# A two-block, four-layer forward pass: the join of the even and the odd layer in token halves, and three pieces of work moved off GpSimd

## What is computed

```python
for l in range(2):                       # first block
    hn = rms_norm(h, attn_norm[l])
    proj = hn @ w_in[l]
    mix = concat(rwkv7_mixer(...), retention_mixer(...), mla_mixer(...))
    h = h + mix @ w_out[l]
    h = h + ffn(rms_norm(h, ffn_norm[l]))
h = rms_norm(h, final_norm)
# second block
h = h + rms_norm(even_mixer(rms_norm(h, even_pre)) @ even_w_out, even_post)
h = h + rms_norm(odd_mixer(rms_norm(h, odd_pre)) @ odd_w_out, odd_post)
# odd_mixer begins with  rms_norm(h, odd_pre) @ odd_w_in   (q, k, v, gates)
```

## Time and profile before

| what | value |
|---|---|
| median of 3 runs | 2005.17 us (2004.16 to 2005.29) |
| profiled execution, its own time | 2005.63 us |
| its span, first to last instruction | 2003.8 us |
| PE busy | 1939.0 us, 97% |
| DVE / ACT / POOL busy | 1112.7 / 825.2 / 72.3 us |
| chain that ended last | PE 87%, DVE 9%, ACT 2%, issue 1%, DMA 1% |
| mean granted TensorE clock | 0.993 |

### The profile page before, as it was taken

How to read it: one execution, slowest core, us unless ns; L and a number is a source line. 1 busy time by engine, 2 the same in 40 slices (tenths; PEclk the granted TensorE clock), 3 DMA queues, 4 the chain that set the end, 5 groups by cost and what they waited for, 6 DMA issues and landing times.

```text
span 2003.8 us, 28013 instructions
## 1 busy us (share of the span) xinstructions
PE 1939.0 (97%) x11924; PEld 1558.9 (78%) x11924; DVE 1112.7 (56%) x1551; ACT 825.2 (41%) x1178; POOL 72.3 (4%) x47
## 2 busy tenths in 40 slices
PE   7998889999999999988999999999999999899998
PEld 6875678888888888647788888887788777689887
DVE  7568745543444544876544334447766674342474
ACT  4247524321222313774432222236554654335273
POOL 4010100000000000110000000000000000020000
PEclk9999999999999999999999999999999999999999
DMA  5340013223322323101122232233222222213102
GB/s 214 106 121 1 4 43 105 87 83 114 105 85 82 118 86 109 55 1 46 64 98 86 87 120 90 80 96 144 86 83 104 86 68 101 105 46 106 63 12 84
DMA packets 27500, 168.95 MB, mean 84 GB/s; under 512 B 3376, under 2 KB 3632, under 8 KB 12144
## 3 DMA queue, kind: packets, MB, share of 16 engines
q1 hardware_dynamic: 27376, 167.16, 24.2%
HBM read 161.77 MB, written 2.10 MB: 82 GB/s over the span
## 4 chain that ended last, share of the span: by engine, by line
PE 87%; DVE 9%; ACT 2%; issue 1%; DMA 1%; SPq 0%; POOL 0%; DVEq 0%; ACTq 0%; POOLq 0%
PE accumulators L698 25%; PE accumulators L700 25%; PE accumulators L699 25%; PE accumulators L724 4%; DVE ring_low L2072 1%; PE accumulators L838 1%; ACT ring_high L1514 1%; PE accumulators L980 1%; DVE accumulators L2318 1%; DVE arena L2331 1%; PE accumulators L946 1%; PE accumulators L929 1%; DVE arena L2382 1%; PE accumulators L1379 1%; DMA ring<-slabs_in 1%
## 5 line engine op out<-in xcount | busy, mean ns | idle before, releaser
L698 PE MATMUL accumulators<-arena_split,ring_high 128*128 128x512 f32 x2164 | 856.4, 396 | 22.1 <-DVE ring_low L2174 10.4
L699 PE MATMUL accumulators<-arena_split,ring_high 128*128 128x512 f32 x2164 | 845.0, 390 | 0.0
L700 PE MATMUL accumulators<-arena_split,ring_low 128*128 128x512 f32 x2164 | 844.9, 390 | 0.0
L698 PEld LDWEIGHTS accumulators<-arena_split,ring_high 128*128 128x128 f32 x2164 | 408.1, 189 | 117.4 <-issue 13.9
L699 PEld LDWEIGHTS accumulators<-arena_split,ring_high 128*128 128x128 f32 x2164 | 408.2, 189 | 87.8 <-issue 4.8
L700 PEld LDWEIGHTS accumulators<-arena_split,ring_low 128*128 128x128 f32 x2164 | 408.0, 189 | 85.5
L1514 ACT ACTIVATE ring_high<-ring 128x2048 fp32r<-128x2048 f32 (+3 forms) x161 | 281.3, 1748 | 414.1 <-PE accumulators L700 412.2
L2072 DVE TENSOR_TENSOR ring_low<-ring,ring_high 128x2048 fp32r<-128x2048 f32 (+3 forms) x161 | 338.5, 2103 | 186.0 <-ACT ring_high L1514 185.2
L1532 ACT ACTIVATE arena<-accumulators 128x512 f32<-128x512 f32 x72 | 43.1, 598 | 277.2 <-DVE accumulators L2053 277.2
L2053 DVE TENSOR_TENSOR accumulators<-accumulators,rstd 128x512 f32<-128x512 f32 x72 | 50.3, 698 | 119.2 <-PE accumulators L700 119.2
L2536 DVE TENSOR_TENSOR arena<-arena,accumulators 128x512 f32<-128x512 f32 x44 | 30.2, 687 | 119.7 <-PE accumulators L700 118.1
(11 more groups left out here) (357 smaller groups left out, 1764.7 us busy)
## 6 DMA issues: line engine op xcount, KB each, us to landing
ring<-slabs_in SPq DMA_DIRECT2D x115, 1024.0 KB, 4.8
ring<-slabs_in SPq DMA_DIRECT2D x38, 704.0 KB, 4.0
ring<-slabs_in SPq DMA_DIRECT2D x4, 576.0 KB, 3.7
h<-x_in SPq DMA_DIRECT2D x4, 512.0 KB, 7.5
con<-con_in SPq DMA_DIRECT2D x1, 2048.0 KB, 9.2
arena<-arena SPq DMA_DIRECT2D x8, 256.0 KB, 4.1
out<-arena SPq DMA_DIRECT2D x8, 256.0 KB, 2.0
ring<-slabs_in SPq DMA_DIRECT2D x2, 768.0 KB, 4.3
```

The costliest lines, as they stand in the source:

```text
L698: pe.matmul(out, weight[0], right[0], start=start, stop=False)
L699: pe.matmul(out, weight[0], right[1], start=False, stop=False)
L700: return pe.matmul(out, weight[1], right[0], start=False, stop=stop)
```

## The change

Four edits. At the start, ACT squares the eight input tiles and DVE adds them; POOL has no part in it, and ACT's copy of `in0_lo_mq0` stands before the second sine. The rotary key is spread to the heads by eight DMAs of SP, before the slab `out{l}_0`. In the decays, DVE makes the decayed keys in place of POOL, and the decayed queries move behind the first level's masked copies. At the joint, the last output tile and the first four odd groups are multiplied in halves of 256 tokens, and the squares, the norm's sum, root, parts and products go by halves; DVE and ACT prepare `odd_qk1` within the first half's tiles.

```diff
+        TOKENS = (slice(0, T // 2), slice(T // 2, T))
@@ PE, joint
-            for m in range(DT):
+            for m in range(DT - 1):
...
-            norm_sum("even_post")
+            def half_norm_sum(half):
+                ts = TOKENS[half]
+                pe.wait_ge(squares_summed, cnt.next(squares_summed))
+                b = group(("ss", "even_post", half), "act")
+                pe.matmul(b[:, ts], cst("ones"), A(51)[:, 0, ts], start=True, stop=True).then_inc(psum_ready, 1)
+            w = split_tiles(split_slab(f"even_out{DT - 1}"), 0, 2 * DT)
+            for half, ts in enumerate(TOKENS):
+                b = open_bank(("eo", DT - 1, half))
+                for n, k in enumerate(EVEN_ORDER):
+                    mm = product(b[:, ts], w[k], tuple(x[:, ts] for x in mix[k]), n == 0, n == 2 * DT - 1)
+                    if half and n == SUM_AFTER:
+                        half_norm_sum(0)
+                enter(("eo", DT - 1, half), "act")
+                mm.then_inc(psum_ready, 1)
...
             for k in range(DT):
                 parts_step(k)
                 for n in range(2):
-                    odd_product(n, k)
-                odd_product(*later.pop(0))
-            for n, k in later:
-                odd_product(n, k)
+                    odd_product(n, 0, k)
+                if k == 2:
+                    half_norm_sum(1)
+            later = [(n, half, k) for half in range(2) for k in range(DT) for n in (2, 3)]
+            for n, half, k in later[:2 * DT]:
+                odd_product(n, half, k)
+            del later[:2 * DT]
+            for k in range(DT):
+                parts_step(k)
+                for n in range(2):
+                    odd_product(n, 1, k)
+                if k < 4:
+                    odd_product(*later.pop(0))
+            for n, half, k in later:
+                odd_product(n, half, k)
-            pair("odd_qk2", [("qk", 4), ("qk", 5)], ["dve"] * 2, None, odd_norm_sum)
+            pair("odd_qk2", [("qk", 4), ("qk", 5)], ["dve"] * 2)
+            odd_norm_sum()
@@ ACT, start
+                    for m in range(DT):
+                        f(A(INPUT_SQUARES + m)[:, 0, :], h[:, m, :], ACT.Square).then_inc(cnt.up(input_square_ready), 1)
                     prepare(f"in{l}_k")
                     for n in range(2):
+                        if n:
+                            prepare(f"in{l}_v")
                         act.wait_ge(angle_ready, cnt.next(angle_ready))
...
-                    prepare(f"in{l}_v")
@@ ACT, joint
+            last_output(0)                                  # square and copy of one half
+            half_root(0)
             for m in range(DT):
+                odd_high(m, 0)                              # high part and square of one half tile
+                if m == 1:
+                    last_output(1)
+                if m == 2:
                     prepare("odd_qk0")
+                if m == 4:
+                    half_root(1)
             for m in range(DT):
+                odd_high(m, 1)
@@ DVE, start: after the first angle
+                        if n == 0:
+                            sum_input_squares()             # seven additions of 512 columns
@@ DVE, decays
                     tt(A(29, 2), A(29, 2), A(35, 2), MUL).then_inc(cnt.up(gram_inputs_ready), 1)
-                    tt(A(10, 2), A(10, 2), A(27, 2), MUL).then_inc(cnt.up(r_decayed), 1)
-                    dve.wait_ge(k_decayed, cnt.next(k_decayed))
+                    tt(A(12, 2), A(12, 2), A(35, 2), MUL).then_inc(cnt.up(k_decayed), 1)
...
+                def queries_decayed():
+                    tt(A(10, 2), A(10, 2), A(27, 2), MUL).then_inc(cnt.up(r_decayed), 1)
+                    retention_output(0)
-                spread_beside = {0: lambda: retention_output(0), 1: lambda: retention_output(1), 3: mixed_lows}
+                spread_beside = {0: queries_decayed, 1: lambda: retention_output(1), 3: mixed_lows}
@@ DVE, joint
+            last_square(0)
+            odd_input(0, {3: lambda: last_square(1), 4: lambda: prepare("odd_qk0")})
+            odd_input(1, {})
@@ POOL
-            for m in range(DT):
...
-                    pool.tensor_tensor(sq, h[:, m, :], h[:, m, :], ALU.mult).then_inc(cnt.up(pool_done), 1)
...
-                pool.tensor_copy(A(31, 8)[64:96], src.broadcast_to((32, 8, T))).then_inc(cnt.up(krope_spread), 1)
-                pool.tensor_tensor(A(12, 2), A(12, 2), A(35, 2), ALU.mult).then_inc(cnt.up(k_decayed), 1)
+            for half, ts in enumerate(TOKENS):
+                for m in range(1, DT):
...
@@ SP, before slab out{l}_0
+                if where is spread_slot:
+                    sp.wait_ge(psum_ready, finished(("rg", l, 1)))
+                    sp.wait_ge(krope_ready, l + 1)
+                    for hd in range(MLA_H):
+                        sp.dma_start(A(31 + hd)[64:96], A(30)[64:96]).then_inc(krope_spread, 16)
```

162 lines of the change are left out of this document (98 added, 64 removed).

## The result

| | before | after |
|---|---|---|
| median of 4 executions each, same chip | 2004.66 us (2003.70 to 2005.29) | 1994.02 us (1991.63 to 1996.54) |
| ratio | | 0.994, 95% interval 0.9923 to 0.9957 |
| profiled execution, its span | 2005.63, 2003.8 us | 1991.63, 1989.8 us |
| mean granted clock of the profiled one | 0.993 | 0.998 |

The change makes the kernel 10.6 us faster by the medians; the forecast was 7.3 us. The median lies in the recorded range (1992.5 to 2001.8) but under the forecast's own bracket of 1996 to 1999.6. The two profiled executions are 14.0 us apart, since the time of one and the same kernel moves by several microseconds with the mean granted clock of the execution, as the four times of after show. The experiments measure this.

What follows compares the result with a forecast made beforehand. TensorE, with work in flight for 97% of the span, was taken to bound the kernel. Terms -3.8-1.6-0.7-1.2 = -7.3 us, from 2005.63 less a further 0.46, gave 1997.8 us; forecast 1996 to 1999.6, range 1992.5 to 2001.8.

Steps and rivals of the forecast that it cites:

- rival 1: Decays: GpSimd's carried-key product doesn't collide with VectorE's L2399 and L2402; that part gives -4.1 us, total 1994.4 us; chance 0.20.
- B: Rotary keys at the beginning of attention: waits of 0.4 and 1.2 us go, -1.6 us (bounds 0 and -3).
- C: Decays, both layers: 2.05 us gained at the gram wait, 1.7 lost again per layer, -0.7 us (bounds -4.1 and 0).
- A: Start: the 2.06 us wait for in0_lo's split and 1.7 us of low-clock loss go, -3.8 us (bounds 0 and -4).
- D: Joint between even and odd layer: 10.7 us of idling and low clock becomes 9.5, -1.2 us (bounds -4 and +3).
- the cover of 4 us: Start: VectorE's split of in0_lo ends at 42.6 us, while PE wants it at 46.7 us.
- Rival 3: Start: VectorE, with seven more sums, still reaches in0_lo's split after 46.7 us; no gain there, 2001.6 us; chance 0.10.
- I take no more than the gaps: Attention: the keys' gain counted only as PE's first waits, 0.38 us in layer 0 and 1.21 in layer 1.
- the collision: Decays: GpSimd's 1.91 us carried-key product is released as L2399 starts and holds up L2402, costing 1.7 us per layer.
- The half matmuls: Joint: 256-column matmuls spaced 0.120 us, 0.0134 us of it fixed; 144 more of them cost +1.9 us.
- rival 4: Joint: slower, low clock until the four groups are done, a half matmul taking 0.213 us; up to 2012.9 us; chance 0.04.
- rival 2: Joint: another wait, longer low clock or weight loads replace the old wait; 0 to +3 us, 1999 to 2002 us; chance 0.16.

Runs made afterwards that it cites:

- the second comparison: The changed kernel itself measured again, nothing altered: median 1995.25 us, 11.5 us under the kernel before on the same chip.
- queries_last: The changed kernel with retention_output(0) ahead of the decayed queries: median 1991.39 us, 0.9919 of the kernel before.
- joint_only: The kernel before with only the token halves at the joint: median 2005.15 us, 0.9991 of the kernel before.
- no_joint: The changed kernel with the joint as before (whole tiles, one norm): median 1994.66 us, 0.9932 of the kernel before.
- sum_earlier: The changed kernel with the matmul of the first half's squares after the fourth instead of the eighth tile (SUM_AFTER 3 for 7): median 1993.88 us, 0.9929 of before.
- start_only: The kernel before with only the start's edit: median 2005.12 us, 0.9983 of the kernel before.
- no_keys: The changed kernel with the rotary keys spread by GpSimd's copy as before: median 1996.12 us, 0.9938 of the kernel before.

## Why the prediction was right, and where not

Sum of the edits by the stages: 4.0 + 3.7 + 1.8 + 1.1 = 10.6 us; the forecast had 3.8 + 1.6 + 0.7 + 1.2 = 7.3. That the medians of the first comparison differ by 10.6 too is luck to the tenth: the second comparison gave 11.5, and at equal clock it is 8.0. The time of 1994.0 lies within the range, not in the forecast's bracket, and near rival 1's 1994.4; rival 1 is not what happened. The 3.3 us between 7.3 and 10.6 are B's 2.1, C's 1.1 and A's 0.2, less 0.1 of D, and that their sum comes near rival 1 is luck.

- **A, the start: right.** 4.0 for 3.8. The two terms (the wait of 2.06 us and the low clock behind it) are both gone, and the cover of 4 us was there: VectorE's split was 0.25 us earlier than worked out. Rival 3 fell.
- **B, the keys: the largest miss, 2.1 us.** The step that failed is "I take no more than the gaps". PE's first waits in layer 0 were 0.38, 0.39, 0.27 and 0.63 us; they became 0, 0, 0.34 and 0.45. In layer 1 the 1.21 us and the three behind it went the same way. The delay of VectorE and ScalarE was handed down over four units. By the spacing of PE's starts the four places gave 0.54, 0.55, -0.07 and 0.18 us, 1.20 in all (from the last score ahead of each to the transpose: 0.97 to 0.43, 0.66 to 0.11, 0.65 to 0.72, 1.12 to 0.94). The first matmul behind each of the two waits that are gone gave 0.06 us, and the scores and products ahead of them 0.11. That is 1.43 of the 1.46 us, and layer 1, whose first wait was 0.83 us longer, comes to 2.26 for 2.25 this way. The idle time in brackets is shorter than what a wait costs, since it counts from the modelled end of a matmul. Even the bound of 3 us was too small. The DMAs cost nothing, as said; they took 4.94 us to issue where the estimate had 5.83.
- **C, the decays: mechanism right, two terms mis-sized.** The gain was 2.16 us for 2.05, and the collision cost 1.30 and 1.34 us for 1.7: I took 0.2 us off the 1.91, and 0.6 is what it was. L2483 lost 1.5 us and VectorE had some 0.2 of slack. Net 0.9 per layer for 0.35. Rival 1 (no collision) fell, in the trace and by queries_last.
- **The clock behind the gram wait wasn't in the sum.** The earlier trace rows hold no window there; the granted 0.66 and 0.77 of before would have been worth 1.1 us to the profiled execution, though not to every one.
- **D, the joint: right in mechanism, near in its terms.** The stage gave 0.9 to 1.8 us for 1.2. The terms of the sum are distances between starts, and by these the first wait cost 0.79 us for 0.8 (1731.11 to 1732.02, less 0.12), and the split 3.54 for 3.5 (1735.34 to 1738.88, with the second half's norm matmul in it). VectorE's pace cost 0.25 and 0.64 us before tiles 1 and 2. Behind the split PE took 3.85 us for six products (1738.88 to 1742.73) that take 2.16 at full clock. Of these 1.7 us, by my estimate, some 0.9 would have been VectorE's pace anyway, since its tiles came no faster; so the pace is 1.8 us for 2.2, and 0.8 is the clock's for 1.1. With 1.9 for the matmuls the sum is 8.8 us against 9.5, and 10.7 less 8.8 is within 0.2 of the 1.8 us of this trace. In the traces with 6.8 us of low clock it is 0.8 us less.
- **The half matmuls: right.** Their spacing is 0.120 us at full clock (1744.17 to 1745.97 us are 15 of them), as worked out from the earlier trace rows, though those two rows give 0.13 us and not the third figure; at the low clock it is 0.213 us (1741.45 to 1742.73 are 6), as rival 4 had it. By the Trainium skill's fixed 2.5 ns ("TensorE: Matmul & The Clock Gate", section Wait — 56ns, not 53.3ns?) a half matmul at full clock would take 0.109; the trace doesn't agree.
- **Rivals 2 and 4** fell in the first trace: the clock was low for 3.4 us there (6.8 in two of the later traces), not until the four groups were done. In the times of joint_only and no_joint the joint's gain doesn't show, which is rival 2's result by another way, with the reserve that equal clock reads low there.

What stays open: why the same wait is followed by low clock in one execution and not in the next; what makes the executions at 0.991 and less, 37 of 93 with the old decays and 0 of 61 with the new; which of the start's two parts gives the 4.0 us; and whether the halves at the joint are the cause of the low clock 155 us later.

## What to carry to other kernels

Where an engine was late at the head of a pipeline, count the later units' waits too, not only the first: the delay goes down the chain, here over four units. When work is moved to free GpSimd, look which of its remaining instructions is released by the moved one, and put it beside operations that read an accumulator bank: one swapped line gave 2.6 us. A gap's price is its length plus a chance of half clock behind it; compare kernels by stages at full clock, which mostly repeated to 0.05 us here (the joint's, whose last wait ran from 5.58 to 6.20 us in before's code, did not), and by mean clock, before a microsecond is believed.

## What the runs showed of the hardware

- The same kernel's times spread over up to 10 us (before 2002.4 to 2012.8), most of it clock: 1.36 us for each 0.001 of mean granted clock explains 86% of the variance within the kernels. About 1 us is left; among the traces, the norm's matmul starts anywhere from 38.1 to 41.0 us.
- A wait of 2.64 us was followed by low clock in two traces and by none in two others of the same code (layer 0); one of 1.65 us was followed by it in sum_earlier and not in after (1.64 us); waits of 0.4 to 1.2 us in a thinly filled stretch were followed by it in start_only and not in no_keys.
- Of a collision both sides pay: GpSimd's product, which began beside VectorE's L2480, took 2.28 us, else 1.91, and VectorE's L2483 behind L2480 took 2.20, else 0.69.
- A half matmul of 256 columns took 0.120 us at full clock and 0.213 us at the low one, start to start.
